# Four RMS norms of a two-block transformer: statistics on token columns, spread by a product with the identity

## The reference

```
u * rsqrt(mean(u * u, axis=-1) + 1e-6) * g
```

## Time and profile before

| | us |
|---|---|
| median of 3 runs (lowest, highest) | 1805.06 (1804.69, 1805.51) |
| the profiled execution | 1816.87 |
| its span, first to last instruction | 1815.0 |
| PE busy | 1741.5 |
| DVE, ACT, POOL busy | 853.6, 692.2, 330.5 |
| mean granted clock of TensorE | 0.973 |

### The profile page before, as it was taken

The page is one execution under the profiler, slowest core; times in us unless marked ns, Lnnn a source line. Parts: engine busy times, 40 slices in busy tenths (PEclk is TensorE's granted clock), DMA queues, the critical chain, the costliest instruction groups (busy, mean ns, idle before and its releaser), DMA issues. The chain is left out here.

```text
span 1815.0 us, 24435 instructions
## 1 busy us (share of the span) xinstructions
PE 1741.5 (96%) x9056; PEld 1432.6 (79%) x9056; DVE 853.6 (47%) x1449; ACT 692.2 (38%) x1190; POOL 330.5 (18%) x259
## 2 busy tenths in 40 slices
PE   6999999999999999998999989999999999999996
PEld 4988888888888888888887777777787788888884
DVE  5325555534445333347546565444454553535353
ACT  5225555533333222266445654322444321212121
POOL 1026666333330000033103331000200200000002
PEclk8999999699999999999999999999999999999998
DMA  7322121023333222236532110223421222222221
GB/s 303 111 76 64 52 69 54 33 99 117 116 119 134 95 94 95 99 106 235 220 107 80 52 47 24 93 93 107 195 70 47 93 93 93 93 93 92 93 93 47
DMA packets 30497, 181.32 MB, mean 100 GB/s; under 512 B 3432, under 2 KB 5864, under 8 KB 11216
## 3 DMA queue, kind: packets, MB, share of 16 engines
q1 hardware_dynamic: 22136, 150.12, 23.7%
q10 hardware_dynamic: 8280, 30.09, 4.7%
HBM read 169.57 MB, written 10.50 MB: 99 GB/s over the span
## 5 line engine op out<-in xcount | busy, mean ns | idle before, releaser
L336 PE MATMUL acc<-rarena,wh 128*128 128x512 f32 (+1 forms) x1928 | 762.6, 396 | 14.6 <-DVE farena L1770 3.6
L337 PE MATMUL acc<-rarena,wh 128*128 128x512 f32 (+1 forms) x1928 | 751.1, 390 | 0.0
L338 PE MATMUL acc<-rarena,wl 128*128 128x512 f32 (+1 forms) x1928 | 751.0, 390 | 0.0
L336 PEld LDWEIGHTS acc<-rarena,wh 128*128 128x128 f32 x1928 | 366.7, 190 | 99.7 <-issue 12.2
L338 PEld LDWEIGHTS acc<-rarena,wl 128*128 128x128 f32 x1928 | 364.7, 189 | 82.8
L337 PEld LDWEIGHTS acc<-rarena,wh 128*128 128x128 f32 x1928 | 365.1, 189 | 77.4 <-issue 0.5
L242 DVE TENSOR_TENSOR wl<-raw,wh 128x2048 fp32r<-128x2048 f32 x113 | 259.0, 2292 | 278.0 <-ACT wh L236 278.0
L236 ACT ACTIVATE wh<-raw 128x2048 fp32r<-128x2048 f32 x129 | 246.1, 1908 | 187.9 <-PE acc L338 172.6
L2077 POOL COPY farena<-farena 128x512 f32<-128x512 f32 x5 | 4.3, 862 | 839.7 <-ACT farena L1402 318.7
L370 PE MATMUL acc<-wh,rarena 128*128 128x256 f32 x384 | 109.9, 286 | 9.1 <-DVE rarena L1417 6.1
L1417 DVE TENSOR_TENSOR rarena<-T,rarena 128x512 fp32r<-128x512 f32 (+3 forms) x128 | 72.9, 574 | 77.7 <-ACT rarena L981 53.5
(11 more groups left out here) (261 smaller groups left out, 1812.9 us busy)
## 6 DMA issues: line engine op xcount, KB each, us to landing
raw<-in_w SPq DMA_DIRECT2D x129, 1024.0 KB, 4.9
early<-in_wmod SPq DMA_DIRECT2D x8, 1024.0 KB, 19.9
farena<-in_gate ACTq DMA_DIRECT2D x4, 1024.0 KB, 4.9
mkv_scratch<-rarena ACTq DMA_DIRECT2D x2, 2048.0 KB, 11.7
rarena<-mkv_scratch ACTq DMA_DIRECT2D x1, 4096.0 KB, 21.5
farena<-in_rpb ACTq DMA_DIRECT2D x16, 240.0 KB, 3.6
farena<-in_x_grid SPq DMA_DIRECT2D x2, 1024.0 KB, 8.2
o_scratch<-farena ACTq DMA_DIRECT2D x8, 256.0 KB, 5.5
```

The source lines that it names most:

```text
L336: mm(o, w[0], m[0], start=start, stop=False)
L337: mm(o, w[0], m[1], start=False, stop=False)
L338: return mm(o, w[1], m[0], start=False, stop=stop)
```

## The change

Three statistics (tokens at the start, y, final norm) and the ctx one are now made with tokens on partitions. `column_sums` takes 128 squares' columns as the stationary operand and moves a few columns of `unit`, a 7-column tile that is 0 but for its fourth column: block b's sums land in column b, the other columns get zeros added. ACT's root and DVE's reciprocal (`invert`) then work on 128x4 (128x2 for ctx), and `spread` broadcasts one such column as the stationary operand and moves the identity, block by block, so that a 128x512 tile in PSUM has the value on every partition. The fourth norm keeps only the column form and spreads it behind FL; ACT copies it to `rstd`. In the final norm PE sums `acc_sq` after seven tiles and adds the eighth tile's squares itself; the spread is made twice, in S0 for DVE and in T0, which ACT copies for POOL. DVE takes six output tiles, POOL two, and the stores' order changes. At the start ACT's `ctx_hi(0)` comes after row copy 3 and `ctx_hi(2)` after all of them; DVE scales token tiles 4 and 5 before it makes modulation 3.

```diff
-DVE_LAST = 5
+DVE_LAST = 6
+        ncol, ncol_c = small[:, 101:105], small[:, 105:107]
+        unit = small[:, 167:174]
...
-            for k in sorted(range(KT), key=lambda k: (k % DVE_LAST, k)):
+            for k in (0, 1, 2, 6, 3, 4, 7, 5):
...
+            def column_sums(bank, src, blocks, first, last_src):
+                for b in range(blocks):
+                    last = mm(bank[:, 0:blocks], src[:, 128 * b:128 * b + 128], unit[:, 3 - b:3 - b + blocks],
+                              start=first and b == 0, stop=last_src and b == blocks - 1)
+                return last
+
+            def spread(bank, cols, blocks):
+                for b in range(blocks):
+                    last = mm(bank[:, 128 * b:128 * b + 128], cols[:, b:b + 1].broadcast_to([128, 128]), ident[:],
+                              start=True, stop=True)
+                return last.then_inc(s_("spread_done"), 1)
...
-                mm(S[1][:, 0:CTX], ones[:], sq0[k % 4][:, 0:CTX], start=k == 0, stop=k == KT - 1).then_inc(s_("acc0_done"), 1)
+                column_sums(S[1], sq0[k % 4], 2, k == 0, k == KT - 1).then_inc(s_("acc0_done"), 1)
...
-                mm(S[0][:], ones[:], sq0[2 * j % 4], start=j == 0, stop=j == KT // 2 - 1).then_inc(s_("acc0_done"), 1)
+                column_sums(S[0], sq0[2 * j % 4], 4, j == 0, j == KT // 2 - 1).then_inc(s_("acc0_done"), 1)
+                if j == 1:
+                    pe.wait_ge(s_("ncol_ready"), 1)
+                    spread(S[1], ncol_c, 2)
+            pe.wait_ge(s_("ncol_ready"), 2)
+            spread(S[0], ncol, 4)
...
+            def spread_y():
+                pe.wait_ge(s_("ncol_ready"), 3)
+                spread(S[0], ncol, 4)
...
-                    tiles_job(0, 2, base, 2, g, hm, CTX)
+                    tiles_job(0, 2, base, 2, g, hm, CTX, between=spread_y if c == 1 else None)
...
-                    norm_sum(S[0], acc_sq[:]).then_inc(s_("sum_done"), 1)
+                    column_sums(S[1], acc_sq, 4, True, True).then_inc(s_("sum_done"), 1)
...
-                    norm_sum(S[0], acc_sq[:])
-                    for b in range(4):
-                        last = mm(S[1][:, b:b + 1], acc_sq[:, 128 * b:128 * b + 128], one1, start=True, stop=True)
-                    last.then_inc(s_("sum_done"), 1)
+                    column_sums(S[1], acc_sq, 4, True, True).then_inc(s_("sum_done"), 1)
...
+            pe.wait_ge(s_("ncol_ready"), 4)
+            spread(S[0], rcol, 4)
...
-            pe.wait_ge(s_("acc4_done"), KT)
-            norm_sum(S[0], acc_sq[:]).then_inc(s_("sum_done"), 1)
+            pe.wait_ge(s_("acc4_done"), KT - 1)
+            column_sums(S[1], acc_sq, 4, True, False)
+            pe.wait_ge(s_("sqx_ready"), 3 * KT)
+            column_sums(S[1], sq, 4, False, True).then_inc(s_("sum_done"), 1)
+            pe.wait_ge(s_("ncol_ready"), 5)
+            spread(S[0], ncol, 4)
+            spread(T[0], ncol, 4)
...
+                if n == 3:
+                    ctx_hi(0)
                 if n == 4:
-                    ctx_hi(0)
                     token_hi(0)
                 if n == 5:
                     ctx_hi(1)
                 if n == 6:
-                    ctx_hi(2)
                     token_hi(1)
+            ctx_hi(2)
...
-            act.wait_ge(s_("rcol_ready"), 1)
+            act.wait_ge(s_("ncol_ready"), 4)
             acc_wait_ready(act, 0, 2, GB["FL"])
+            act.wait_ge(s_("spread_done"), 4)
+            f(rstd, S[0][:], ACT.Copy).then_inc(s_("rstd_ready"), 1)
...
-            f(rstd, S[0][:], ACT.Sqrt, scale=1.0 / D, bias=eps).then_inc(s_("rms_ready"), 1)
+            f(ncol, S[1][:, 0:4], ACT.Sqrt, scale=1.0 / D, bias=eps).then_inc(s_("rms_ready"), 1)
+            act.wait_ge(s_("spread_done"), 6)
+            f(rstd, T[0][:], ACT.Copy).then_inc(s_("rstd_ready"), 1)
...
+            def invert(cols, sem_value):
+                v.wait_ge(s_("rms_ready"), sem_value)
+                nc.vector.reciprocal(cols, cols).then_inc(s_("ncol_ready"), 1)
...
             sum_pair(2)
-            scale_ctx(0, 1)
             sum_pair(3)
-            link(scale_ctx(2, 3, 4, 5, 6, 7))
+            v.wait_ge(s_("spread_done"), 1)
+            link(scale_ctx(0, 1, 2, 3, 4, 5, 6, 7))
             rms_reciprocal(1)
+            v.wait_ge(s_("spread_done"), 2)
...
-                    reciprocal_of(1, S[0][:])
+                    invert(ncol, 3)
+                    v.wait_ge(s_("spread_done"), 3)
...
-            reciprocal_of(2, rstd)
-            v.wait_ge(s_("rms_ready"), 3)
-            nc.vector.reciprocal(rcol, rcol).then_inc(s_("rcol_ready"), 1)
+            invert(rcol, 4)
+            v.wait_ge(s_("ncol_ready"), 4)
...
             acc_wait_ready(v, 0, 2, g)
+            v.wait_ge(s_("rstd_ready"), 1)
...
-            v.wait_ge(s_("rms_ready"), 6)
-            nc.vector.reciprocal(rstd, rstd).then_inc(s_("rstd_ready"), 1)
-            v.wait_ge(s_("rstd_ready"), 1)
+            invert(ncol, 7)
+            v.wait_ge(s_("spread_done"), 5)
             for k in range(DVE_LAST):
-                stt(y[:, k], y[:, k], vec(P_FIN + k), rstd, MUL, MUL).then_inc(s_("final_ready"), 1)
+                stt(y[:, k], y[:, k], vec(P_FIN + k), S[0][:], MUL, MUL).then_inc(s_("final_ready"), 1)
...
+            nc.gpsimd.memset(unit, 0.0).then_inc(s_("consts_ready"), 1)
+            gp.wait_ge(s_("consts_ready"), 2)
+            nc.gpsimd.memset(unit[:, 3:4], 1.0).then_inc(s_("consts_ready"), 1)
```

More of the change, by code:

```diff
@@ L88, in build @@
         ones = sb("ones", [128, 128])
-        small = sb("small", [128, 168])
+        small = sb("small", [128, 176])
         F_KB, R_KB = 29.5, 128
@@ L376, in norm_sum @@
                 return mm(bank[:, 0:n], ones[:], src, start=True, stop=True)
-            pe.wait_ge(s_("consts_ready"), 3)
+            def column_sums(bank, src, blocks, first, last_src):
[8 more added lines that the diff above has]
+                return last.then_inc(s_("spread_done"), 1)
+            pe.wait_ge(s_("consts_ready"), 5)
             for k in range(KT):
                 pe.wait_ge(s_("sq0_ready"), k + 1)
-                mm(S[1][:, 0:CTX], ones[:], sq0[k % 4][:, 0:CTX], start=k == 0, stop=k == KT - 1).then_inc(s_("acc0_done"), 1)
+                column_sums(S[1], sq0[k % 4], 2, k == 0, k == KT - 1).then_inc(s_("acc0_done"), 1)
             for j in range(KT // 2):
                 pe.wait_ge(s_("pair_summed"), j + 1)
-                mm(S[0][:], ones[:], sq0[2 * j % 4], start=j == 0, stop=j == KT // 2 - 1).then_inc(s_("acc0_done"), 1)
+                column_sums(S[0], sq0[2 * j % 4], 4, j == 0, j == KT // 2 - 1).then_inc(s_("acc0_done"), 1)
[4 more added lines that the diff above has]
+            spread(S[0], ncol, 4)
             pe.wait_ge(s_("silc_ready"), 4)
@@ L883, in root @@
             def root(x):
-                bank, w = ((S[1], CTX), (S[0], SEQ))[x]
+                cols, bank = ((ncol_c, S[1][:, 0:2]), (ncol, S[0][:, 0:4]))[x]
                 act.wait_ge(s_("acc0_done"), (KT, KT + KT // 2)[x])
-                f(bank[:, 0:w], bank[:, 0:w], ACT.Sqrt, scale=1.0 / D, bias=eps).then_inc(s_("rms0_ready"), 1)
+                f(cols, bank, ACT.Sqrt, scale=1.0 / D, bias=eps).then_inc(s_("rms_ready"), 1)
             def ctx_hi(i):
@@ L902, in _ @@
             token_squares(range(0, 4))
-            act.wait_ge(s_("consts_ready"), 3)
+            act.wait_ge(s_("consts_ready"), 4)
             root(0)
@@ L1141, in _ @@
                     act.wait_ge(s_("sum_done"), 1)
-                    f(S[0][:], S[0][:], ACT.Sqrt, scale=1.0 / D, bias=eps).then_inc(s_("rms_ready"), 1)
+                    f(ncol, S[1][:, 0:4], ACT.Sqrt, scale=1.0 / D, bias=eps).then_inc(s_("rms_ready"), 1)
                 if c == 4:
@@ L1432, in _ @@
             v.wait_ge(s_("silc_ready"), 2)
-            v.wait_ge(s_("consts_ready"), 4)
+            v.wait_ge(s_("consts_ready"), 6)
             nc.vector.tensor_copy(silc32[:, :, 0:2], silc.rearrange("p (k s) -> p k s", s=2)).then_inc(s_("silc_ready"), 1)
@@ L1438, in rms_reciprocal @@
             def rms_reciprocal(x):
-                bank, w = ((S[1], CTX), (S[0], SEQ))[x]
-                v.wait_ge(s_("rms0_ready"), x + 1)
-                link(nc.vector.reciprocal(bank[:, 0:w], bank[:, 0:w]))
+                invert((ncol_c, ncol)[x], x + 1)
             def sum_pair(j):
@@ L1499, in _ @@
             token_rows(1)
+            token_scale(2)
+            modulation(3)
             ctx_rows(2)
-            modulation(3)
-            token_scale(2)
             ctx_rows(3)
@@ L1572, in attend_nb @@
                             v.wait_ge(s_("bm_done"), g + 1 + a)
-                            v.wait_ge(s_("consts_ready"), 5)
+                            v.wait_ge(s_("consts_ready"), 7)
                             v.sem_inc(s_("bias_done"), 1)
@@ L1883, in _ @@
             split_job(v, 0, 2, JB["QM"] + 1)
-            reciprocal_of(4, rstd)
+            reciprocal_of(5, rstd)
             def qm_tile(n, x):
```

(11 more changed lines are left out.)

## The result

| | before | changed | |
|---|---|---|---|
| first comparison, median of 11 and 10 executions | 1805.51 us | 1797.5 us | -8.0 us |
| ratio | | 0.9929 | 95% interval 0.9906 to 0.9952 |
| profiled execution (span) | 1816.87 (1815.0) us | 1793.58 (1791.4) us | -23.3 us |

One execution of the changed kernel took 2953.14 us at a mean granted clock of 0.68, the only one of its kind on record; it is left out of the ten, and why it came is not known.

What follows compares the result with a forecast made beforehand. TensorE, busy for 96% of the span, was taken as the bound, so norms cost only where it waits. End -5.3, fourth norm -1.7, third +0.4, start -1.5 sum to -8.1 us: median 1797.0 us, range 1792.8 to 1804.5.

Steps and rivals of the forecast that it cites:

- The end: Final norm to last store: narrow root and reciprocal, a spread, earlier output tiles; -5.3 us, bounds -3 and -6.
- the end pays half: Rival at the final norm: spread 2.0 us at half clock, tiles 1.3 us beside POOL; 1799.3 us, chance 0.12.
- the slow row: Old final tiles, both operands in SBUF, beside POOL; by it VectorE's six tiles would cost 7.8 us, not 4.3.
- The fourth norm: At FL and V2: sum replaced by spread, PE's waits for two accumulators go; -1.7 us, bounds -0.6 and -2.5.
- The third norm: At MKV: the spread waits behind a tile of 24 products; +0.4 us, bounds 0 and +1.2.
- The start: Before V: wide reciprocals go, two spreads come, V starts at 41 to 44; -1.5 us, bounds -3.8 and +5.7.
- half-clock rival: At the start, two: half clock until V, 1804.2 us, chance 0.15; through V's first job, 1816.1 us, chance 0.06.
- I carry its difference over to the median unchanged: Whole span: the profiled execution's 11.8 us above the median of 1805.06 us was kept as a fixed offset.

Runs made afterwards that it cites:

- lower group: Executions of the kernel before from 1798.8 to 1810.7 us, median 1805.8 us; its other executions lie from 1811.1 to 1822.2 us.
- the start alone: Kernel before with only the start's change (statistics and both orders): median 1804.3 us against 1805.8, 1 of 12 executions over 1811 us.

## Why the prediction was right or wrong

Over all profiles, by sections between weight splits, old way against new way:

| section | forecast | old | new | difference |
|---|---|---|---|---|
| end, from the last split | -5.3 | 39.0 (9 profiles) | 33.9 (11) | -5.1 |
| FL and V2's start | -1.7 | 39.4 (9) | 37.8 (11) | -1.6; its part behind the first split, at full clock in every profile, 26.9 and 24.8: -2.1 |
| third norm, MKV | +0.4 | 37.35 without half clock (7) | 37.7 (7) | +0.3; all profiles with the old way 38.05 (13): -0.4 |
| start: V's first product | -1.5 | 42.3 (8) | 41.5 (10) | -0.8; at the split behind V's jobs 117.9 and 117.5: -0.4 |

The changed places add up to some 7.5 us in the profiles (5.1, 2.1 and 0.4 to 0.8, less 0.3), the medians of the lower groups to 9.0. The rest is not located: the sections that the change doesn't touch vary by 2 to 6 us between profiles. From the split behind V2's start to the 27th after it, for one, the changed kernel took 408.0 to 408.4 us in three profiles, kernels with most of the old norms 408.4 to 413.3 in ten, with more or less half clock in it.

- **The end: right.** Spread 1.16 us (1.1), tiles 0.66 from start to start (0.72), stores as worked out. The lead in the first pair was 5.4 us. Part of the rival *the end pays half* came true in some executions: in the changed kernel's second profile the clock was half there, and its end was 1.5 us longer (34.9 against 33.4). The tiles stayed at 4.04 us. The rule that I weighed against the slow row (the Trainium skill, "SBUF — State Buffer", section "Who interferes with whom") held: 0.74 us a tile beside POOL, with one SBUF input, against 1.75 with two.

```profile
1785.87 2.07 PE L388 MATMUL S<-ident,small 128*128 128x128 f32 x8 [0.57 <-DVE small L1459]
1787.73 1.73 PE L388 MATMUL T<-ident,small 128*128 128x128 f32 x8
1787.98 4.04 DVE L2004 SCALAR_TENSOR_TENSOR farena<-farena,par,S 128x512 f32<-128x512 f32 x6 [2.17 <-PE S L388]
```

- **The fourth norm: right in mechanism, low by 0.4 us.** Both waits of L370 are gone; of PE's waits from 855 to 885 us the line below is all that is left (columns as in the earlier trace rows). Sum, spread and the two waits came to -1.5, and I had added 0.2 more; the runs show 2.1, and where the other 0.4 comes from is open.

```profile
PE S L382 <- POOL farena L2115: 0.2, 1, 0.2
```

- **The third norm: right.** +0.3 where I had +0.4, from the spread waiting behind a tile of 24 products; PE's longest wait there is 1.3 us now, 1.7 before. Not foreseen: 6 of 13 profiles with the old norm had 3.4 us of half clock in that section, which made it 1.5 us longer, none of 7 with the new one; that pays the 0.3 back.
- **The start: right in place, not in what the lead was measured from.** Row products at 24.5 (24.3), V at 39.9 to 42.7 us where I had 40 to 44, and the start alone gave -1.5 in the lower group as forecast. But kernels with the old start vary as much (V from 40.3 to 43.1 in eight profiles), so neither the 41.85 of the first profile nor the full lead was typical, and of the 1.5 the profiles show only 0.4 to 0.8: that the size came out is in part luck. Neither half-clock rival's time occurred.
- **The step that failed** is the first one: "I carry its difference over to the median unchanged". The profiled execution's 11.8 us over the median were no offset to be carried. They were one stretch with a place, 334 to 371 us, and by their times and clocks four of ten executions have it. With the offset held fixed, the sum had no term for that stretch going away: it stood at nothing, without a reason. The granted clock along the whole span, rather than at the places of the change alone, shows 37.5 us at half clock in a pair whose predecessors from 133 us on had none. Then the question "does anything in this change shift when that pair is reached?" would have stood among the rivals. Its price, by the groups that the later runs showed, was -11.4 x 0.41 = -4.7 us on the mean. Together with the -9.0, which alone lies well inside my range, that makes -13.7 us; over all comparisons the means stand at 1810.3 and 1796.7 us, 13.6 apart. That the medians of the first comparison met my forecast is in part luck: six of the eleven executions of the kernel before fell into the lower group, and with five the median would have been in the upper one.

## What to carry to other kernels

Read the granted clock over the whole span before costing a change, and ask which group of executions the profile belongs to: a median of three and one profile can stand for different ones. When a change "gains" in a stretch it does not touch, run its common scaffolding (allocations, constants, waits) alone; here that separated 9.0 us between like groups, some 7.5 of them found in the places that were changed, from 4.7 us of luck. A norm's row statistics on 4 columns, spread by a product with the identity (1.05 us), beat a 3.35 us reciprocal only where something waits for it: at the end fully, in the middle by the waits it frees.

## What the runs showed of the hardware

- **An execution can fall to half clock for a whole attention pair or not, with the same instructions.** 11.4 us between the groups. In the two profiles that have it PE was busy nearly all the time at half clock and returned to full at 371.5 and 371.8 us, among 512-column products that follow the pair; in a third (332.9 to 343.1 us) it returned inside the pair.
- **Added wide products did not bring the full clock back.** With twelve of them beside the start's sums, PE was busy for all of the 23 us from 7 to 30 and by its products' times stayed at half until about 30 us (1.92 us for two of 512 columns at 28.22, 1.10 at 31.09); in the kernel before, which has only such wide sums, it was full from about 10 us (1.03 us for four at 10.05).
- **32 bytes of shift in SBUF cost 0.09 us a pair**, 0.5 us over six, in most profiles; why is not known.
- **V's pace varies between executions**, 65.9 us for four jobs once and 67.7 to 69.2 otherwise, at full clock. Unexplained.
